# First loads split and reordered, x turned tile by tile into eight banks, second bias summed in four row groups, ple inputs turned in the routing stage

## Chip, cores, metric

One core of a Trainium2 chip. The metric is the device time of one execution in microseconds. TensorE is called PE, VectorE DVE, ScalarE ACT, GpSimd POOL and SyncE SP.

## What is computed

One hybrid layer on 256 prompt tokens and 8 samples of 8 tokens (320 tokens, model width 1024, all float32), with a final norm. Cut to what matters:

```
h = rmsnorm(x, norm1_g);  z = h @ w_in              # 8208 columns, cut into the inputs of the branches
qkv, new_buf = short_conv(qkv_pre, conv_buf, conv_w)  # conv_buf: the last 3 rows of every sample
y_a = gated delta rule branch;  y_b = chunk MLP branch
x = x + (sigmoid(m_a) * y_a + sigmoid(m_b) * y_b) @ w_out
h2 = rmsnorm(x, norm2_g)
x = x + moe_ffn(h2)      # 32 experts, top 4, blocks of 64 rows; each block: act(xe @ w1[e] + b1[e]) @ w2[e] + b2[e], times its gate
h3 = rmsnorm(x, norm3_g)
x = x + sigmoid(h3 @ ple_gate_w) * (p @ ple_w)
y = rmsnorm(x, final_norm_g)
```

Because the gates multiply b2[e] too, the kernel adds it once for all tokens: gates (tokens x 32) times b2 (32 x 1024).

## The kernel before

The program is written engine by engine, with semaphores set by hand. All of SBUF is one array ("arena") in which regions are used again in later stages; PSUM is one array ps of 8 banks of 512 words, and pj[0], pj[1] are its banks 0 and 1. Tokens form three tiles: two of 128 (prompt) and one of 64 (samples).

**Start.** SP issues its loads in one queue (L407 to L421): x (prompt, samples), all constants (725 KB, the identity matrix in their first 128 columns), the small rows that are transposed into per-partition columns (conv_w, three norm gains, dn_norm_g), the convolution state (288 KB), then the first 2 MB chunk of w_in, the small gate weights with two broadcasts, and the second chunk. Every later chunk waits until the chunk two before it has been used (L423 to L426). ACT takes the sum of squares of each tile (rms), DVE normalises it (L1441 to L1450) and copies the turned rows out of PSUM (L1451). PE waits for constants and rows (L645, L646), turns the rows (L647), then the convolution state in 24 transposes of 24 rows (L648 to L652), then x: for each of 8 blocks of 128 columns three transposes, one per tile, into bank k % 2, and ACT or DVE copies each bank out, scaled by norm1_g, into hT (L1204, L1456). So block k waits until block k - 2 has been copied:

```
            for k in range(KD):
                ...
                elif k >= 2:
                    pe.wait_ge(sem(("hT_ready", "hT_odd_ready")[k % 2]), k // 2)
                for tt, (t0, tn) in enumerate(TILES):
                    m = pe.transpose(pj[k % 2][:, t0:t0 + tn], x[0:tn, tt, k * P:(k + 1) * P], ident[0:tn, 0:tn])
```

When hT is complete (L690, L691), 24 feature products follow (L692), each of 8 matmuls of 320 columns; a float32 matmul is two passes in the trace. POOL, ACT and DVE do the short convolution behind them. All products go through the helper at L642.

**Middle.** The rest of the projections runs between the steps of the delta rule. SP reloads x for the residual (L459, L460) just before the chunks of w_proj_b (L461). In the routing stage (L938 to L988) h2 is transposed, the router logits are computed (bank 7) and transposed, x is put into banks 0 to 4 by identity products (L961, L1089) as the start of the output sum, and DVE works out ranks, block tables and gates. gmT (L1817) holds the gates with experts on 32 partitions. SP then waits for the tables (L486) and issues the loads of the experts' weights, each waiting for the slot to be used (L489 to L495).

**Expert blocks.** For each block of 64 rows PE does the select, hidden, second product and combine; combine (L995) adds a block's rows to banks 0 to 4 as 18 bfloat16 matmuls.

**End.** After the last block SP loads ple_gate_w and ple_w (L499 to L504), then b2, the ple inputs and the final norm gain (L506 to L509), which share one semaphore. PE waits for them (L1107), does the products of gates and b2 (L1108 to L1112, K = 32 rows), the last combine (L1113), and turns the ple inputs (L1115 to L1118). DVE copies the sum out of PSUM (L1865 to L1868), the norm of each tile follows (samples first), PE turns it (turn_h3, L1143), and the ple products (L1135) and gate logits (L1138) are done in the order of L1153 to L1179. ACT and DVE close with sigmoid, product, norm and store.

## Time and profile before

| what | value |
|---|---|
| median of 3 runs | 1649.81 us (1649.1 to 1650.41) |
| the profiled execution | 1651.6 us, span 1649.8 us |
| PE busy | 1595.5 us (97%) |
| DVE, ACT, POOL busy | 518.9, 327.0, 105.1 us |
| DMA | 477.23 MB, mean 289 GB/s |
| mean granted PE clock | 0.987 |

The profile gives times from the span's start. A busy PE is not PE at its peak, so the rows further on give counts of passes with their time, and the chain of waits tells what each stretch ended on. Matmuls and weight loads (PEld) overlap.

### The profile page before, as it was taken

The page shows a single profiled execution, that of the slowest core. Times are in us where ns is not written, and L with a number is a line of the kernel's source. Part 1 is how long each engine was busy: PE and PEld are TensorE (multiplying, and loading weights), DVE is VectorE, ACT ScalarE, POOL GpSimd, SP SyncE. Part 2 cuts the span into 40 slices and gives each one's busy share as a digit, 9 for nine tenths or more (in the row PEclk, how much of TensorE's full clock was granted, in tenths as well). Part 3 has the DMA queues.
Part 4 walks back from the last instruction along what each step waited for, and adds up shares of the span by engine and source line. Part 5 has one row for each costly group of instructions (what it writes and reads, how often), then busy time and mean ns, then how long its engine had stood idle before and what let it go on. Part 6 is the DMA issues. An engine that isn't in the chain of part 4 may idle for free.

```text
span 1649.8 us, 21617 instructions
## 1 busy us (share of the span) xinstructions
PE 1595.5 (97%) x8645; PEld 750.2 (45%) x8646; DVE 518.9 (31%) x1110; ACT 327.0 (20%) x529; POOL 105.1 (6%) x150
## 2 busy tenths in 40 slices
PE   7999999999999999999999999999999999999998
PEld 4667776676575433333333333333333333333333
DVE  3665322134561422222222222222122222222223
ACT  2224222122410131111111111111111111111123
POOL 1321202011103030000000000000000000000000
PEclk9999999999899999999999999999999999999989
DMA  5234321216574659996999999999999969949930
GB/s 162 103 111 135 97 77 56 99 62 207 168 231 148 273 229 427 429 428 262 424 430 427 430 427 429 429 427 430 427 429 428 427 288 407 430 198 419 422 106 32
DMA packets 71936, 477.23 MB, mean 289 GB/s; under 512 B 7914, under 2 KB 18595, under 8 KB 47235
## 3 DMA queue, kind: packets, MB, share of 16 engines
q1 hardware_dynamic: 69414, 467.65, 69.6%
q0 software_dynamic: 2480, 8.98, 1.9%
q8 instruction: 31, 0.51, 0.1%
q14 instruction: 11, 0.09, 0.0%
HBM read 469.73 MB, written 6.62 MB: 289 GB/s over the span
## 4 chain that ended last, share of the span: by engine, by line
PE 73%; DMA 21%; DVE 3%; issue 1%; SPq 1%; ACT 0%; DVEq 0%
PE ps L642 69%; DMA arena<-in_moe_w 20%; PE ps L992 1%; PE ps L1067 1%; PE ps L1012 1%; DMA arena<-in_final_norm_g 1%; DVE arena L1597 1%; PE ps L660 0%; DMA arena<-in_state_conv 0%; DVE arena L1631 0%; DVE arena L1594 0%; PE ps L714 0%; DVE arena L1635 0%; SPq L503 0%; DVE arena L1661 0%
## 5 line engine op out<-in xcount | busy, mean ns | idle before, releaser
L642 PE MATMUL ps<-arena 128*64 128x512 f32 (+9 forms) x8056 | 1499.3, 463 | 31.5 <-DMA arena<-in_moe_w 15.6
L642 PEld LDWEIGHTS ps<-arena 128*64 128x64 f32 (+7 forms) x8056 | 675.8, 143 | 815.9 <-issue 599.8
L1848 DVE TENSOR_SCALAR arena<-ps 128x512 f32<-128x512 f32 x35 | 24.2, 692 | 354.8 <-PE ps L642 354.8
L1395 ACT ACTIVATE arena<-arena 128x512 f32<-128x512 f32 x35 | 22.0, 630 | 413.9 <-DVE arena L1848 413.9
L1401 ACT ACTIVATE arena<-ps,arena 128x512 bf16<-128x512 f32 x35 | 24.1, 688 | 283.2 <-PE ps L642 283.2
L1861 DVE SCALAR_TENSOR_TENSOR arena<-ps,arena 128x512 f32<-128x512 f32 x35 | 26.3, 751 | 126.8 <-ACT arena L1401 126.8
L1820 DVE TENSOR_TENSOR arena<-ps,arena 128x512 f32<-128x512 f32 x36 | 24.9, 692 | 128.7 <-PE ps L992 128.7
L1856 DVE TENSOR_REDUCE arena<-ps 128x1 f32<-128x320 f32 x35 | 17.2, 492 | 95.8 <-PE ps L1012 95.8
L1395 ACT ACT_TABLE_LOAD x35 | 44.9, 1283 | 0.6
L1380 ACT ACTIVATE arena<-ps 128x512 f32<-128x512 f32 x36 | 21.6, 599 | 109.0 <-PE ps L642 109.0
L1481 DVE SCALAR_TENSOR_TENSOR arena<-arena 128x344 f32<-128x344 f32 x48 | 35.6, 741 | 1.7
L1263 ACT ACTIVATE arena<-ps 128x320 f32<-128x320 f32 x32 | 14.0, 436 | 98.3 <-PE ps L642 98.1
L992 PEld LDWEIGHTS ps<-arena 128*128 128x128 f32 x144 | 19.9, 207 | 28.5 <-issue 28.4
L1193 ACT ACTIVATE arena<-arena 128x1024 f32<-128x1024 f32 (+1 forms) x12 | 12.6, 1051 | 97.5 <-DVE arena L1716 91.1
L1863 DVE TENSOR_TENSOR arena<-arena 128x512 bf16<-128x512 f32 x35 | 24.2, 693 | 24.4 <-ACT arena L1403 24.4
L1843 DVE TENSOR_SCALAR arena<-arena 128x128 f32<-128x128 f32 (+1 forms) x105 | 29.6, 337 | 0.0
L1403 ACT ACTIVATE arena<-arena 128x512 bf16<-128x512 f32 x35 | 22.0, 630 | 28.6 <-DVE arena L1861 28.6
L992 PE MATMUL ps<-arena 128*128 128x128 f32 x144 | 26.9, 309 | 0.0
L1575 DVE TENSOR_TENSOR arena<-arena,ps 128x512 f32<-128x512 f32 (+1 forms) x11 | 7.6, 688 | 59.8 <-PE ps L642 59.8
L1067 PE MATMUL ps<-arena 128*128 128x128 f32 x140 | 26.2, 310 | 0.0
L1851 DVE SCALAR_TENSOR_TENSOR arena<-arena 128x512 f32<-128x512 f32 x35 | 24.3, 694 | 1.2
L1854 DVE TENSOR_TENSOR arena<-arena 128x512 f32<-128x512 f32 x35 | 24.3, 693 | 1.2
(256 smaller groups left out, 699.8 us busy)
## 6 DMA issues: line engine op xcount, KB each, us to landing
arena<-in_moe_w SPq DMA_DIRECT2D x192, 2048.0 KB, 19.5
arena<-in_w_in SPq DMA_DIRECT2D x16, 2048.0 KB, 11.0
arena<-in_state_delta POOLq DMA_DIRECT2D x16, 512.0 KB, 6.4
arena<-in_w_proj_a SPq DMA_DIRECT2D x2, 2048.0 KB, 11.1
out_sd_s<-arena SPq DMA_DIRECT2D x8, 512.0 KB, 5.7
arena<-in_w_proj_b SPq DMA_DIRECT2D x2, 2048.0 KB, 11.3
arena<-in_w_out SPq DMA_DIRECT2D x2, 2048.0 KB, 8.0
arena<-in_ple_gate_w SPq DMA_DIRECT2D x2, 2048.0 KB, 15.1
```

Source lines behind the costliest of these rows:

```text
L642: return pe.matmul(out, lhsT, rhs, start=first, stop=last, skip_group_check=True)
L992: m = pe.transpose(ps[:, TURN_B, P * j:P * j + P], xsel_by_k[:, j // 2, j % 2, :], ident)
L1067: m = pe.transpose(ps[:, GATE_B, P * j:P * j + P], a_by_k[:, j, :], ident)
L1395: ACTF(s_sb, g_sb, ACT.Sigmoid, scale=ALPHA).then_inc(sem("glu_sig_ready"), 1)
L1481: ch.link(STT(a, z[:, i:i + CW], g_conv[:, i, n:n + 1], a, ALU.mult, ALU.add))
L1820: TT(xselT.rearrange("p (g j) s -> p g j s", g=2), ps[:, TURN_B, :].rearrange("p (j g s) -> p g j s", j=4, g=2), g2_by_k.rearrange("p (g j ...
L1843: m = TS(Pg[0:tn, tt, :], cst("slot", tn), posb[0:tn, tt, bass.ds(b, 1)], gateb[0:tn, tt, bass.ds(b, 1)], ALU.is_equal, ALU.mult)
L1848: TS(g_sb, ps[:, GATE_B, :], LIMIT, None, ALU.min).then_inc(sem("glu_gate_ready"), 1)
L1851: STT(u_sb, u_sb, 1.0, g_sb, ALU.add, ALU.mult).then_inc(sem("glu_up_ready"), 1)
L1854: TT(a_sb, u_sb, s_sb, ALU.mult).then_inc(sem("act_ready"), 1)
L1861: STT(y_rest, ps[:, UP_B, :], gate_col, y_parts[0], ALU.mult, ALU.subtract).then_inc(sem("ysb_ready"), 1)
L1863: TT(y_parts[2], y_rest, y_parts[1], ALU.subtract).then_inc(sem("ysb_ready"), 1)
```

## The change

At the start x is loaded in three loads with a semaphore each, and only the identity's 128 columns of the constants go ahead; the convolution state and the rest of the constants go behind the first weight chunk, the small gate weights behind the second. PE turns x tile by tile, each block k into bank k, behind the turned rows; the convolution state is turned in groups of four transposes behind products 0 to 5. The first product waits block by block for hT.

The ple inputs and the final norm gain are loaded before x is loaded again, and turned in the routing stage into banks 0 and 1; the identity products take tile 1 first. b2 is loaded four times, to partitions 0, 32, 64 and 96, after the tables are ready, and gmT is copied to the same groups. At the end the b2 products of the two prompt tiles use a row group each; ple products 0, 4 and 1 go around the last combine, and 2 and 3 later.

```diff
-            sp.dma_start(x[:, 0:2, :], t["x_prompt"][0].rearrange("(a p) d -> p a d", p=P)).then_inc(sem("x_in"), 16)
-            sp.dma_start(x[0:64, 2, :], t["x_sample"].rearrange("b s d -> (b s) d")).then_inc(sem("x_in"), 16)
-            sp.dma_start(arena[:, cst_at:cst_at + NCONST], t["consts"]).then_inc(sem("consts_in"), 16)
+            for tt in range(2):
+                sp.dma_start(x[:, tt, :], t["x_prompt"][0, P * tt:P * tt + P, :]).then_inc(sem(f"x_tile{tt}_in"), 16)
+            sp.dma_start(x[0:64, 2, :], t["x_sample"].rearrange("b s d -> (b s) d")).then_inc(sem("x_tile2_in"), 16)
+            sp.dma_start(arena[:, cst_at:cst_at + P], t["consts"][:, 0:P]).then_inc(sem("ident_in"), 16)
...
-            sp.dma_start(sc_rows[0:24, :], t["state_conv"][0].rearrange("b r n -> (b r) n")).then_inc(sem("rows_loaded"), 16)
             for c in range(FRONT_SLOTS):
                 sp.dma_start(slots[c], chunk_src[c]).then_inc(landed[c], 16)
                 if c == 0:
-                    sp.dma_start(wab, w_in[:, :, COL_AB:COL_AB + 16]).then_inc(sem("ab_in"), 16)
-                    sp.dma_start(alog, t["a_log"].broadcast_to([P, H])).then_inc(sem("ab_in"), 16)
-                    sp.dma_start(dtb, t["dt_bias"].broadcast_to([P, H])).then_inc(sem("ab_in"), 16)
+                    sp.dma_start(sc_rows[0:24, :], t["state_conv"][0].rearrange("b r n -> (b r) n")).then_inc(sem("consts_in"), 16)
+                    sp.dma_start(arena[:, cst_at + P:cst_at + NCONST], t["consts"][:, P:NCONST]).then_inc(sem("consts_in"), 16)
+            sp.dma_start(wab, w_in[:, :, COL_AB:COL_AB + 16]).then_inc(sem("ab_in"), 16)
+            sp.dma_start(alog, t["a_log"].broadcast_to([P, H])).then_inc(sem("ab_in"), 16)
+            sp.dma_start(dtb, t["dt_bias"].broadcast_to([P, H])).then_inc(sem("ab_in"), 16)
...
+            sp.wait_ge(sem("S0_stored2"), 32)
+            sp.dma_start(ptok[:, 0:2, :], t["p_prompt"][0, 0].rearrange("(a p) d -> p a d", p=P)).then_inc(sem("ple_in"), 16)
+            sp.dma_start(ptok[0:64, 2, :], t["p_sample"][0].rearrange("b s d -> (b s) d")).then_inc(sem("ple_in"), 16)
+            sp.dma_start(fng, t["final_norm_g"].rearrange("(a d) -> a d", a=1).broadcast_to([P, D])).then_inc(sem("ple_in"), 16)
+            sp.dma_start(x[:, 0:2, :], t["x_prompt"][0].rearrange("(a p) d -> p a d", p=P)).then_inc(sem("x_tile0_in"), 16)
+            sp.dma_start(x[0:64, 2, :], t["x_sample"].rearrange("b s d -> (b s) d")).then_inc(sem("x_tile2_in"), 16)
...
             sp.wait_ge(sem("tables_ready"), 1)
+            for i in range(4):
+                sp.dma_start(b2[32 * i:32 * i + 32, :], t["moe_b2"][0]).then_inc(sem("router_in"), 16)
...
-            sp.wait_ge(used[uslot[3]], nb)
-            sp.dma_start(b2[0:NE, :], t["moe_b2"][0]).then_inc(sem("ple_in"), 16)
-            sp.dma_start(ptok[:, 0:2, :], t["p_prompt"][0, 0].rearrange("(a p) d -> p a d", p=P)).then_inc(sem("ple_in"), 16)
-            sp.dma_start(ptok[0:64, 2, :], t["p_sample"][0].rearrange("b s d -> (b s) d")).then_inc(sem("ple_in"), 16)
-            sp.dma_start(fng, t["final_norm_g"].rearrange("(a d) -> a d", a=1).broadcast_to([P, D])).then_inc(sem("ple_in"), 16)
...
-            pe.wait_ge(sem("consts_in"), 16)
-            pe.wait_ge(sem("rows_loaded"), 16 * 6)
-            pe.transpose(pj[1][:, 0:121], rows_in[0:121, :], ident[0:121, 0:121]).then_inc(sem("rows_turned"), 1)
-            for g in range(6):
+            pe.wait_ge(sem("ident_in"), 16)
+            pe.wait_ge(sem("rows_loaded"), 16 * 5)
+            pe.transpose(ps[:, 7, 384:505], rows_in[0:121, :], ident[0:121, 0:121]).then_inc(sem("rows_turned"), 1)
+            for tt, (t0, tn) in enumerate(TILES):
+                pe.wait_ge(sem("xn_ready"), tt + 1)
+                for k in range(KD):
+                    if tt == 0 and k == 7:
+                        pe.wait_ge(sem("cols_ready"), 1)
+                    m = pe.transpose(ps[:, k, t0:t0 + tn], x[0:tn, tt, k * P:(k + 1) * P], ident[0:tn, 0:tn])
+                    if tt == 2:
+                        m.then_inc(sem("hT_done"), 1)
+
+            def turn_old(g):
+
+                if g == 0:
+                    pe.wait_ge(sem("consts_in"), 32)
                 for i in range(4):
                     f = 4 * g + i
                     m = pe.transpose(ps[:, 2 + g, 24 * i:24 * i + 24], sc_rows[0:24, f * P:(f + 1) * P], ident[0:24, 0:24])
-                m.then_inc(sem("old_done"), 1)
-            pe.wait_ge(sem("xn_ready"), 3)
-            for k in range(KD):
-                if k == 1:
-                    pe.wait_ge(sem("cols_ready"), 1)
-                elif k >= 2:
-                    pe.wait_ge(sem(("hT_ready", "hT_odd_ready")[k % 2]), k // 2)
-                for tt, (t0, tn) in enumerate(TILES):
-                    m = pe.transpose(pj[k % 2][:, t0:t0 + tn], x[0:tn, tt, k * P:(k + 1) * P], ident[0:tn, 0:tn])
-                m.then_inc(sem("hT_done"), 1)
+                m.then_inc(sem("rows_turned"), 1)
...
                 for k in ks:
+                    if n == 0:
+                        pe.wait_ge(sem(("hT_ready", "hT_odd_ready")[k % 2]), k // 2 + 1)
                     last = mm(pj[n % 2][:, 0:TOK], slots[c % FRONT_SLOTS][:, k, m * P:(m + 1) * P], rhs[:, k, :], k == 0, k == KD - 1)
...
-            pe.wait_ge(sem("hT_ready"), KD // 2)
-            pe.wait_ge(sem("hT_odd_ready"), KD // 2)
             for n in range(FT):
                 features(n, n // 4, n % 4, hT)
+                if n < 6:
+                    turn_old(n)
...
+            def turn_p(k):
+
+                for tt, (t0, tn) in enumerate(TILES):
+                    m = pe.transpose(ps[:, P_BANKS[k], t0:t0 + tn], ptok[0:tn, tt, k * P:(k + 1) * P], ident[0:tn, 0:tn])
+                m.then_inc(sem("pT_done"), 1)
+
+            pe.wait_ge(sem("ple_in"), 48)
+            turn_p(0)
             pe.wait_ge(sem("hT_odd_ready"), KD + 1)
             for k in range(KD):
                 m = mm(ps[0:NE, 7, SEQ:TOK], rw[:, k, :], h2T[:, k, SEQ:TOK], k == 0, k == KD - 1)
             m.then_inc(sem("logits_done"), 1)
+            turn_p(1)
             pe.wait_ge(sem("logitT_ready"), 1)
             for tt, (t0, tn) in enumerate(TILES):
                 m = pe.transpose(ps[0:tn, 6, NE * tt:NE * tt + NE], logitT[0:NE, t0:t0 + tn], ident[0:NE, 0:NE])
             m.then_inc(sem("logits_done"), 1)
 
-            for tt in range(2):
+            for tt in (1, 0):
+                if tt == 0:
+                    pe.wait_ge(sem("pT_ready"), 2)
                 for g in range(2):
                     mm(ps[:, 2 * tt + g, :], ident, x[:, tt, 512 * g:512 * g + 512], True, True)
...
-            pe.wait_ge(sem("ple_in"), 64)
-            for tt in range(2):
-                for g in range(2):
-                    mm(ps[:, 2 * tt + g, :], gmT[0:NE, P * tt:P * tt + P], b2[0:NE, 512 * g:512 * g + 512], False, True)
-            for g in range(2):
-                mm(ps[64 * g:64 * g + 64, 4, :], gmT[0:NE, 2 * P:TOK], b2[0:NE, 512 * g:512 * g + 512], False, True)
-            combine(nb + 1)
-            pe.wait_ge(sem("xselT_ready"), nb + 1)
-            for k in range(2):
-                for tt, (t0, tn) in enumerate(TILES):
-                    m = pe.transpose(ps[:, P_BANKS[k], t0:t0 + tn], ptok[0:tn, tt, k * P:(k + 1) * P], ident[0:tn, 0:tn])
-            m.then_inc(sem("pT_done"), 1)
...
-            pe.wait_ge(sem("pT_ready"), 2)
+            pe.wait_ge(sem("router_in"), 16 * 8)
+            pe.wait_ge(sem("rankT_ready"), 3)
+            for tt in range(2):
+                for g in range(2):
+                    q = 32 * (2 * tt + g)
+                    mm(ps[:, 2 * tt + g, :], gmT[q:q + NE, P * tt:P * tt + P], b2[q:q + NE, 512 * g:512 * g + 512], False, True)
+            for g in range(2):
+                mm(ps[64 * g:64 * g + 64, 4, :], gmT[0:NE, 2 * P:TOK], b2[0:NE, 512 * g:512 * g + 512], False, True)
+            ple_product(0)
+            combine(nb + 1)
             ple_product(4)
+            ple_product(1)
             pe.wait_ge(sem("xn_ready"), 7)
             turn_h3(2)
-            ple_product(0)
             for half in range(2):
                 pe.wait_ge(landed[uslot[half]], 16 * (before[uslot[half]] + NE + 1))
             pe.wait_ge(sem("hT_odd_ready"), KD + 2)
             pe.wait_ge(sem("xn_ready"), 8)
             turn_h3(0)
             gate_logits(4, range(KD // 2, KD))
-            ple_product(1)
+            ple_product(2)
             pe.wait_ge(sem("hT_odd_ready"), KD + 4)
             gate_logits(0)
             pe.wait_ge(sem("ple_added"), 1)
             pe.wait_ge(sem("xn_ready"), 9)
             turn_h3(1)
-            ple_product(2)
             ple_product(3)
```

DVE copies the turned rows before tile 1's norm, copies a group of the convolution state before its convolution of product n < 6 (keep_old), and copies gmT to partitions 32, 64 and 96 after the tables. ACT copies the turned ple inputs before the exponential of the gates (L1375).

## Rows read from the trace of the kernel before

**Rows 1.** The page: the chain that ended last, shares of the span.

```profile
PE 73%; DMA 21%; DVE 3%; issue 1%; SPq 1%; ACT 0%; DVEq 0%
```

**Rows 2.** Chain of the first 60 us: start, duration (us), what.

```profile
4.49 7.03 DMA arena<-in_state_conv
...
12.09 2.68 PE ps L651 x24
14.77 7.31 PE ps L660 x24
...
22.77 37.44 PE ps L642 x127
```

**Rows 3.** Timeline of the first 45 us: start, duration, what, idle before.

```profile
1.84 0.57 SPq L409 DMA_DIRECT2D arena<-in_consts  x1
...
4.83 0.40 SPq L417 DMA_DIRECT2D arena<-in_w_in  x1
...
23.43 0.34 PEld L642 LDWEIGHTS ps<-arena 128*128 128x128 f32 x1 [0.20 <-issue]
...
28.74 16.39 PEld L642 LDWEIGHTS ps<-arena 128*128 128x128 f32 x61 [0.17 <-issue]
```

**Rows 4.** Timeline of the last 110 us: start, duration, what, idle before.

```profile
1543.34 3.65 PE L642 MATMUL ps<-arena 128*64 128x512 f32 x16
...
1565.42 0.98 PEld L642 LDWEIGHTS ps<-arena 64*128 64x128 bf16 x12 [0.41 <-issue]
...
1567.60 1.22 PEld L642 LDWEIGHTS ps<-arena 128*64 128x64 bf16 x14 [0.41 <-issue]
...
1580.36 11.80 PE L642 MATMUL ps<-arena 32*128 32x512 f32 x30 [1.44 <-DMA arena<-in_final_norm_g]
...
1581.13 0.69 DVE L1863 TENSOR_TENSOR arena<-arena 128x512 bf16<-128x512 f32 x1 [0.69 <-ACT arena L1403]
...
1592.10 1.21 PE L1117 MATMUL ps<-arena 128*128 128x128 f32 x6
...
1597.09 0.71 PE L1149 MATMUL ps<-arena 64*128 64x64 f32 x8 [0.90 <-DVE arena L1446]
...
1603.23 1.09 PE L1149 MATMUL ps<-arena 128*128 128x128 f32 x8
...
1617.40 24.20 PE L642 MATMUL ps<-arena 128*128 128x512 f32 x56
```

**Rows 5.** Stretches: length, busy (count) of PE, PEld, DVE, ACT, POOL; clock, DMA, GB/s.

```profile
1581.60:1583.00 1.40, 1.40 (x3) 0.65 (x2) 0.23 (x1) 1.01 (x2) 0.00 (x0) 0.56 0.00 0
...
1590.00:1592.00 2.00, 2.00 (x10) 0.36 (x6) 0.00 (x0) 0.00 (x0) 0.00 (x0) 0.50 0.00 0
```

**Rows 6.** DMA issues of the first 60 us: KB each, us to landing.

```profile
arena<-in_w_in SPq DMA_DIRECT2D x3, 2048.0 KB, 11.8
...
arena<-in_consts SPq DMA_DIRECT2D x1, 725.5 KB, 7.5
```

**Rows 7.** Stretches at the start, columns as in rows 5.

```profile
12.00:13.00 1.00, 1.00 (x11) 0.98 (x10) 0.84 (x3) 0.00 (x0) 0.00 (x0) 1.00 1.04 383
```

**Rows 8.** Chain of the expert loop.

```profile
962.12 24.80 DMA arena<-in_moe_w
986.97 3.68 PE ps L642 x16
```

**Rows 9.** Timeline of SP's queue in the middle.

```profile
466.11 0.67 SPq L426 DMA_DIRECT2D arena<-in_w_proj_b  x1
...
487.32 0.37 SPq L426 DMA_DIRECT2D arena<-in_w_proj_b  x1
```

**Rows 10.** Timeline of the routing stage and the first block.

```profile
564.98 1.09 PE L642 MATMUL ps<-arena 128*32 128x64 f32 x16 [0.78 <-DVE arena L1737]
...
583.61 0.17 DVE L1830 CAST arena<-ps 1x32 int32<-1x32 f32 x1
...
595.19 15.92 SPq L495 DMA_DIRECT2D arena<-in_moe_w  x5
```

More of the change, by code:

```diff
@@ L310, in hybrid_layer @@
         ple_moved = y_rest[0:64]
-        assert mo[0] <= small_at, (mo[0], small_at)
+        print("margin", small_at-mo[0], "small", small_at+1100-sm[0]); assert mo[0] <= small_at, (mo[0], small_at)
         def part_of(tt, i):
@@ L1203, in _ @@
                 act.wait_ge(sem("hT_done"), k + 1)
-                ACTF(hT[:, k, :], pj[k % 2][:, 0:TOK], ACT.Copy, scale=g1[:, k:k + 1]).then_inc(sem("hT_ready"), 1)
+                ACTF(hT[:, k, :], ps[:, k, 0:TOK], ACT.Copy, scale=g1[:, k:k + 1]).then_inc(sem("hT_ready"), 1)
             def silu_part(n):
@@ L1373, in _ @@
             turned((4, 5))
+            for k in range(2):
+                act.wait_ge(sem("pT_done"), k + 1)
+                ACTF(pT[:, k, :], ps[:, P_BANKS[k], 0:TOK], ACT.Copy).then_inc(sem("pT_ready"), 1)
             act.wait_ge(sem("top_ready"), 1)
@@ L1406, in _ @@
             ACTF(warm, eps_col, ACT.Sqrt)
-            act.wait_ge(sem("pT_done"), 1)
-            for k in range(2):
-                ACTF(pT[:, k, :], ps[:, P_BANKS[k], 0:TOK], ACT.Copy).then_inc(sem("pT_ready"), 1)
             for i, tt in enumerate(TAIL_TILES):
@@ L1455, in _, with keep_old @@
                 dve.wait_ge(sem("hT_done"), k + 1)
-                TS(hT[:, k, :], pj[k % 2][:, 0:TOK], g1[:, k:k + 1], None, ALU.mult).then_inc(sem("hT_odd_ready"), 1)
-            for g in range(6):
-                dve.wait_ge(sem("old_done"), g + 1)
-                dve.tensor_copy(oldT[:, 4 * g:4 * g + 4, :], ps[:, 2 + g, 0:96].rearrange("p (f j) -> p f j", f=4)).then_inc(sem("old_turned"), 1)
+                TS(hT[:, k, :], ps[:, k, 0:TOK], g1[:, k:k + 1], None, ALU.mult).then_inc(sem("hT_odd_ready"), 1)
+            def keep_old(g):
+                dve.wait_ge(sem("rows_turned"), g + 2)
+                dve.tensor_copy(oldT[:, 4 * g:4 * g + 4, :], ps[:, 2 + g, 0:96].rearrange("p (f j) -> p f j", f=4)).then_inc(sem("cols_ready"), 1)
             def samples(w):
@@ L1473, in _ @@
             for n in range(FT):
+                if n < 6:
+                    keep_old(n)
                 evacuated(dve, n)
@@ L1834, in _ @@
             nb = dve.value_load(tab[0:1, 96 + NE - 1:96 + NE], min_val=1, max_val=MAXB)
+            for i in range(1, 4):
+                m = dve.tensor_copy(gmT[32 * i:32 * i + 32], gmT[0:32])
+            m.then_inc(sem("rankT_ready"), 1)
             dve.wait_ge(sem("part_ready"), 6)
```

30 lines of the change are left out of this document (14 added, 16 removed).

## The prediction

> **What bounds the kernel now.** I read the chain of waits first. Over the whole span it is TensorE for 73% and DMA for 21% [rows 1]. The edit sits at the two ends and in the routing stage, so the question for each part is what holds those stretches, and whether a shift of the start reaches the end.
>
> At the start PE does nothing until the last row load, the one of the convolution state, has landed; then come 24 small transposes (2.68 us), 24 transposes of x held back by two PSUM banks (7.31 us), and at 22.77 the first product. After that the chain is PE without a break past 60 us [rows 2]. The first products run slowly: a weight load of one pass takes 0.34 us after 0.20 idle, so one starts every 0.53, and from 28.74 on 61 of them take 16.39 us, 0.27 each [rows 3]. So the array is at 1.2 GHz until 28.7 and at 2.4 after it.
>
> At the end PE stands idle 1.44 us for the final norm gain's load, issued behind the bias and the ple inputs; the second bias and the last combine then run until 1592.1 [rows 4]. From 1581.8 on, the granted clock is 0.50, the lower level [rows 5]. After the combine comes a norm of the last tile that PE waits out, then a solid block of products, from 1617.40 for 24.2 us [rows 4].
>
> **The start, part by part.** (1) *Loads.* PE now waits for x, 64 KB of identity and the small rows instead of all constants and the convolution state. Constants landed 7.5 us after their issue at 1.84, so at 9.34 [rows 3, 6]; of their 725 KB 661 move away, 1.8 us at the 383 GB/s of a full stretch [rows 7]. I take the rows at 7.9 us: 9.34 less 1.8, plus a little for the split loads (7.5 to 9.4, the full saving or none). Their transpose ends near 8.35. The first weight chunk, 11.8 us after its issue at 4.83, landed at 16.6; 949 KB (constants' rest and convolution state) no longer precede it, 2.5 us, so it lands at 14.1, or up to 0.7 earlier.
>
> (2) *Turning x tile by tile into eight banks.* No transpose waits for a bank now. At 2.4 GHz eight full transposes took 1.09 us and eight 64-row ones 0.71 [rows 4]; at 1.2 GHz I double that: 2.2 + 2.2 + 1.4 = 5.8 us, so PE is through at 14.2. The gains' copy on DVE now stands ahead of tile 1's norm, which still has the 2.2 us of tile 0's transposes to hide in. The first product needs only bank 0's copy, which runs beside the other transposes. First product at 14.3 against 22.77: **8.5 us**.
>
> (3) *Clock.* Before, 5.9 us of products ran at half speed, a loss of 3.0. PE no longer pauses between transposes and products (7.31 after 14.77 is 22.08, then nothing until 22.77 [rows 2]), so I take 0.8 of it back, between -0.8 and 1.3.
>
> (4) *The old rows' transposes* move behind products 0 to 5, four each. At 1.2 GHz they took 2.68 us together. At 2.4 four cost 4 x 0.089 (0.71/8) = 0.36. To this comes the change of row shape: the six ple transposes took 1.21 us [rows 4] where four full and two short ones at the rates above are 4 x 0.136 + 2 x 0.089 = 0.72, so 0.49 for three changes, 0.16 each. Two changes per group, part of it already in the 0.71: 0.55 a group, **3.3 us back** (2.1 to 5). The Trainium skill, page "TensorEngine Tiling (Array Packing)", Tiling Modes, speaks against this part: changing the tiling mode drains the array. The trace agrees, with 0.16 us a change. What these groups wait for (constants' rest, convolution state, near 17) is there before product 0 ends, near 21. The second chunk, now issued right behind the first, is needed at product 4, near 35. The small gate weights behind it are needed at product 24.
>
> Start in sum: 8.5 + 0.8 - 3.3 = **6.0 us**. It carries to the end if the rest moves with it. The one long DMA-bound stretch (from 962, twelve or thirteen experts of 25.5 us DMA and 3.7 PE each [rows 8]) is paced by slots that PE frees; I expect it to shift whole.
>
> **The middle.** On SP the ple inputs and the norm gain (832 KB, three issues) now go ahead of the reload of x and of w_proj_b. That is 2.2 us at 383 GB/s, with the issues 3 to 4 us, for a chunk issued at 466.11; PE needs it when its neighbour is issued, at 487.3 [rows 9]. With 11.8 us for landing it comes at 482: hidden, 5 us over. What queues behind the new wait for a stored state is this same chunk. Turning p (six transposes, 1.21 us) goes into PE's idle time: 0.78 us before 564.98 [rows 10], and a gap while the logits are copied. ACT copies it before an exponential that waits for DVE. I count 0.1 us lost (0 to 0.8). Three copies of gmT run on DVE while it waits for parts. The four loads of b2 follow the tables at 583.8, when SP has nothing until 595.19 [rows 10]: 512 KB, 1.4 us, over before the first expert load. If they did collide, one stall of 1.4 us would appear in the expert loop.
>
> **The end.** PE's last expert product lets the next begin at 1578.85.
> - b2: four full products in a row are 4 x 2 x 0.43 = 3.4 us at 2.4 GHz (56 passes in 24.20). On four row groups I let them run together, as two column halves do: 16 passes in 3.65, 0.23 each [rows 4]. So 0.9 for the four, 0.9 for the sample pair, 0.1 of change. The Trainium skill, "TensorE: Matmul & The Clock Gate", Part 3, gives 3.07 times for four row tiles, not four: the sum would be 0.2 less.
> - ple product 0: 4 x 0.43 = 1.7. Combine may start at 1582.5; its last part is ready at 1581.8 (1581.13 + 0.69), so no idle time.
> - combine at 2.4 GHz: 1565.42 to 1567.60 [rows 4], 2.2 us, and 0.2 of drain. It ends at 1584.9 instead of 1592.1: 7.2 us (wait 1.5, clock 5.0, packing 2.4, less 1.7 put in).
> - The last tile's norm takes 5.0 us as before (1592.1 to 1597.09). PE fills 3.5 of it with ple products 4 and 1; h3's transposes start at 1589.9.
> - Before, ple product 0 (1.7 us) stood behind them; now the logits wait only for DVE's copy, 0.8 us. Together 8.1.
> - One product fewer stands in the rest: 1.7. Together **9.8 us**. ACT's and DVE's closing 8 us stay.
>
> **Sum.** 6.0 - 0.1 + 9.8 = 15.7. The profiled execution took 1651.6, 1.8 outside its span, and would take 1635.9. It stands 1.8 above the median of 1649.8; less 15.7 that gives 1634.1, so **1634.0**.
>
> **Rivals.**
> - *The clock falls in the new gap at the end.* PE now stands idle 1.3 us before the h3 transposes and 0.8 after them. Before, an idle 1.44 us followed by 32-row products preceded the fall [rows 4, 5]. Against: gaps around the same transposes did not lower it before (0.90 ahead of them), and the packed products fill more of the array. A third of the 10.2 us seen costs 1.7, the whole 5.1: 1635.7 to 1639. Chance 0.30.
> - *One end pays less.* Row groups serial (2.5), old-row transposes at their upper bound (1.7), rows landing at 9.4 (1.5): 1639.7 together; or the start's gain is lost whole because DMA paces the experts [rows 8]: 1640. Against: those loads wait for PE. 0.15.
> - *Slower.* The small transposes behind each of the first six products could keep the array at 1.2 GHz, as it was through all transposes before 22 [rows 2, 3]. Six products are 6 x 16 passes of 0.27, 26 us; at half speed 26 more, 2.2 of them counted: 1634 + 23.8 = 1658. It decides if the low clock lasts beyond some 35 us after the first product. Against: each product is 4.3 us without a gap. 0.02.
> - *The edit does nothing there*, since something else held PE: 0.02; the chain names both loads.
>
> **Chances.** Forecast 0.51, clock at the end 0.30, a gain missed 0.15, same 0.02, slower 0.02. 0.2% is 3.3 us, about what runs of this kernel tell from no change; all cases but the last two are faster by more. The range runs from 1629.5 (rows and chunk early 1.0, clock 0.5, old rows at 2.1 another 1.2, and half-speed stretches elsewhere that may shorten as work shifts, 1.8) to 1640.0 (the clock falls, or a gain missed).
>
> **What would show it.** First product near 14.3, with nothing waiting for the convolution state; its pace 0.27 by 20; groups of four small transposes of 0.5 us; no wait of PE for the norm gain; clock 1.00 from 1560 to the last logits; four b2 products together; expert loads where they were against the tables. Wrong if PE waits for the weight chunk at the start, if a DMA wait is new in the expert loop, or if the combine still runs at 0.50.

## The result, and the profile after

The changed kernel took 1640.53 us (median of four runs, 1638.59 to 1642.08), the kernel before 1650.11 beside it (1649.1 to 1650.53): ratio 0.9953, interval 0.9936 to 0.9971. Forecast were 1634.0 and a range from 1629.5 to 1640.0. The direction is right; of 15.7 us forecast 9.6 came. Later, on another chip, the same two gave 1637.57 and 1646.73, ratio 0.9938 (0.9925 to 0.9952).

The profiled execution took 1640.53 (span 1638.7; before 1651.6 and 1649.8). From here on A is the kernel before and B the changed one. The timeline of B's start, columns as in [rows 3]:

```profile
4.71 0.42 SPq L416 DMA_DIRECT2D arena<-in_w_in  x1
5.17 0.53 SPq L418 DMA_DIRECT2D arena<-in_state_conv  x1
5.74 0.53 SPq L419 DMA_DIRECT2D arena<-in_consts  x1
6.32 1.35 SPq L416 DMA_DIRECT2D arena<-in_w_in  x1
7.71 8.78 SPq L420 DMA_DIRECT2D arena<-in_w_in  x1
8.05 0.43 PE L649 MATMUL ps<-arena 121*128 121x121 f32 x1 [8.05 <-DMA arena<-in_dn_norm_g]
8.29 4.53 PE L655 MATMUL ps<-arena 128*128 128x128 f32 x24
12.42 1.93 DVE L1469 TENSOR_SCALAR arena<-ps,arena 128x320 f32<-128x320 f32 x4 [1.91 <-PE ps L655]
18.00 6.92 PE L644 MATMUL ps<-arena 128*128 128x320 f32 x16 [5.19 <-DMA arena<-in_w_in]
24.85 0.42 PE L665 MATMUL ps<-arena 24*128 24x24 f32 x4
...
29.72 0.43 PE L665 MATMUL ps<-arena 24*128 24x24 f32 x4
```

The small rows came at 8.05, close to the forecast 7.9, and x was turned by 12.8, earlier than the forecast 14.2. Then PE stands idle for 5.19 us, for the first weight chunk. The chain of the start says the same:

```profile
4.71 13.25 DMA arena<-in_w_in
...
18.00 6.92 PE ps L644 x16
```

The chunk landed 13.25 us after its issue, at 17.96: later than before (16.6, [rows 3, 6]), though 949 KB that went ahead of it now stand behind it. DMA traffic in two stretches of before and then of after (columns as in [rows 5]; the last two are the busy share of the DMA engines and GB/s; the clock column reads 1.00 up to the first recorded change, in B at 12.5, so ahead of that the clock's level is read from the pace of the passes):

```profile
7.00:11.00 4.00, 0.00 (x0) 0.00 (x0) 1.52 (x4) 3.45 (x7) 0.00 (x0) 1.00 1.02 287
...
14.00:18.00 4.00, 4.00 (x19) 2.34 (x18) 0.55 (x1) 0.98 (x2) 0.00 (x0) 1.00 0.53 173
```

```profile
7.00:11.00 4.00, 2.94 (x14) 2.98 (x15) 1.92 (x5) 1.38 (x3) 0.00 (x0) 1.00 0.61 211
...
14.00:18.00 4.00, 0.00 (x0) 0.00 (x1) 0.35 (x1) 0.09 (x1) 0.00 (x0) 0.74 0.92 237
```

After the change the engines are only 0.61 busy just when the chunk should stream, and busy with it and its followers when PE waits.

The end, PE's timeline:

```profile
1572.24 13.61 PE L644 MATMUL ps<-arena 128*64 128x512 f32 x62
1586.99 0.71 PE L1154 MATMUL ps<-arena 64*128 64x64 f32 x8 [1.14 <-DVE arena L1459]
1588.57 5.35 PE L644 MATMUL ps<-arena 128*64 128x512 f32 x16 [0.88 <-DVE arena L1898]
...
1608.02 22.48 PE L644 MATMUL ps<-arena 128*128 128x512 f32 x52
```

Its weight loads show the second bias and the combine:

```profile
1575.83 0.31 PEld L644 LDWEIGHTS ps<-arena 32*128 32x128 f32 x8 [0.81 <-issue]
1576.90 0.19 PEld L644 LDWEIGHTS ps<-arena 32*64 32x64 f32 x4 [0.76 <-issue]
1577.90 0.30 PEld L644 LDWEIGHTS ps<-arena 128*128 128x128 f32 x2 [0.81 <-issue]
...
1579.82 0.98 PEld L644 LDWEIGHTS ps<-arena 64*128 64x128 bf16 x12 [0.76 <-issue]
```

And the clock ahead of h3's transposes and behind them:

```profile
1582.00:1588.00 6.00, 4.56 (x22) 1.73 (x20) 4.90 (x7) 4.33 (x10) 0.00 (x0) 1.00 0.00 0
1589.50:1592.80 3.30, 3.30 (x10) 1.14 (x8) 0.00 (x0) 0.00 (x0) 0.00 (x0) 0.50 0.00 0
```

The wait for the norm gain is gone (PE has no idle time ahead of the products at 1575.83); the four bias products take 1.07 us together; the combine runs at full clock from 1579.82. But behind the two idle spells (1.14 and 0.88 us) the clock falls for 3.4 us: sixteen logit passes take 5.35 us instead of the 3.65 of [rows 4].

**Splitting the difference.** The expert stage makes a good mark: the second expert whose weights PE waits for. In before and after:

```profile
1016.34 3.87 PE L642 MATMUL ps<-arena 128*64 128x512 f32 x18 [1.24 <-DMA arena<-in_moe_w]
```

```profile
1013.18 8.23 PE L644 MATMUL ps<-arena 128*64 128x512 f32 x54 [1.24 <-DMA arena<-in_moe_w]
```

Ahead of it the change brought 3.2 us, behind it (633.5 against 625.5 us to the end of the span) 8.0. The same marks of every profile taken (times in us; the mark is the same expert in all):

| profile | first product | second expert wait | from there to end | span |
|---|---|---|---|---|
| A | 22.77 | 1016.34 | 633.5 | 1649.8 |
| A again (e12) | 22.34 | 1014.31 | 633.8 | 1648.1 |
| A third (e13) | 22.12 | 1014.62 | 632.7 | 1647.3 |
| B | 18.00 | 1013.18 | 625.5 | 1638.7 |
| B again (e11) | 17.93 | 1013.18 | 623.6 | 1636.8 |
| B, chunk held alone (e1) | 15.61 | 1013.22 | 625.2 | 1638.4 |
| B, second chunk held (e2) | 17.83 | 1011.50 | 623.7 | 1635.2 |
| B, old rows together (e3) | 18.27 | 1011.59 | 625.3 | 1636.9 |
| B, spells filled (e4) | 19.52 | 1016.77 | 623.7 | 1640.5 |
| the same again (e14) | 18.01 | 1010.84 | 623.8 | 1634.6 |
| B, chunk on ACT's queue (e5) | 19.10 | 1013.06 | 625.3 | 1638.4 |
| three edits (e6) | 18.95 | 1009.27 | 622.9 | 1632.2 |
| B, bias in one row group (e7) | 17.98 | 1010.70 | 627.9 | 1638.6 |
| B's end, A's start (e8) | 22.81 | 1015.45 | 625.5 | 1641.0 |
| held, together, split (e9) | 15.52 | 1008.61 | 622.9 | 1631.5 |
| e9 with halves (e10) | 13.02 | 1008.16 | 622.9 | 1631.1 |

Two things stand in it. In B and its variants the part behind the mark repeats to 0.3 us once it is known whether the clock fell (623.6 to 623.8 without, 625.2 to 625.5 with). The part ahead of it does not: five profiles of B's start (B, B again, e4, e7, e14) lie between 1010.7 and 1016.8. In them the low-clock stretches between 100 and 700 us add up to 24 to 31 us, near the same places but of 3.4, 6.8 or 10.2 us each; with the chunk's landing (18.0 to 19.5) that is part of the spread, not all of it.

### The profile page after: what moved, and what is told of

It is laid out like the page before. It is cut to its first block, busy times and chain, and to the rows that moved or that the text cites. A ratio compares the mean times of both kernels' runs of the same rounds, so it can differ in the third digit from the quotient of the medians.

```text
span 1638.7 us, 21626 instructions
## 1 busy us (share of the span) xinstructions
PE 1586.7 (97%) x8645; PEld 747.7 (46%) x8646; DVE 521.3 (32%) x1113; ACT 327.5 (20%) x529; POOL 105.1 (6%) x150
## 4 chain that ended last, share of the span: by engine, by line
PE 74%; DMA 21%; DVE 3%; issue 1%; ACT 0%; SPq 0%; DVEq 0%
PE ps L644 70%; DMA arena<-in_moe_w 20%; PE ps L1010 1%; PE ps L1085 1%; PE ps L1030 1%; DMA arena<-in_w_in 1%; DVE arena L1612 1%; DVE arena L1646 0%; DVE arena L1609 0%; PE ps L721 0%; DVE arena L1650 0%; DVE arena L1676 0%; DVE arena L1658 0%; DVE arena L1656 0%; PE ps L835 0%
## 5 line engine op out<-in xcount | busy, mean ns | idle before, releaser
L644 PE MATMUL ps<-arena 128*64 128x512 f32 (+9 forms) x8056 | 1494.9, 463 | 33.1 <-DMA arena<-in_moe_w 15.1
L1233 ACT ACTIVATE arena<-ps 128x64 f32<-128x64 f32 x24 | 5.5, 230 | 95.7 <-PE ps L644 95.7
## 6 DMA issues: line engine op xcount, KB each, us to landing
arena<-in_ple_gate_w SPq DMA_DIRECT2D x2, 2048.0 KB, 15.1
```

The source lines that it names most:

```text
L644: return pe.matmul(out, lhsT, rhs, start=first, stop=last, skip_group_check=True)
```

## The experiments

Theory: (1) the chunk came late since what is issued behind it takes from it; rival: a chunk is slow by itself, whatever stands behind it; (2) the clock fell because of the two idle spells.

**e1: everything behind the first chunk waits for it.**

```diff
                 sp.dma_start(slots[c], chunk_src[c]).then_inc(landed[c], 16)
                 if c == 0:
+                    sp.wait_ge(landed[0], 16)
```

> The queue now waits for the first weight chunk before it issues the convolution state, the rest of the constants, the second chunk and all that follows. Theory A (what is issued behind the chunk takes part of the DMA engines while it loads): the chunk lands near 14.2, which is its issue at 4.71 and some 9.5 us, the first product starts near 14.3 and not at 18.00, 3.7 us earlier; the old rows' transposes then wait for the late state and constants (949 KB, issued at 14.3, there near 19), 1 to 2 us given back. Total 1638 to 1640 against 1640.5 of the changed kernel. Theory B (the pace at which one chunk's own 1024 packets of 2 KB go out is what sets its landing, about 11 us as for other weight chunks of this kernel): lands at 15.7 to 16, first product near 16, and after the wait for the old rows no gain in the total. Theory C (nothing behind it matters): 18.0 as now, total longer by 2 us or more.

**e2: only the second chunk and the gate weights wait** (the same line behind the constants' load).

> Only the second weight chunk and the small loads behind it wait for the first chunk; the convolution state and the rest of the constants (949 KB) are issued right behind the first chunk as in the changed kernel. If it was the state and the constants that delayed the first chunk: lands near 17.9 as now. If it was the second chunk and the gate weights: near 14.2 to 15, first product 3 us earlier, old rows there in time, total near 1637.5. If both share: between, near 16.5, total near 1639.

Measured: e1 1638.48 us (0.9927, 0.9902 to 0.9952), e2 1636.86 (0.9929, 0.9908 to 0.9949). PE's timeline in e1 and a stretch of it:

```profile
15.61 7.45 PE L645 MATMUL ps<-arena 128*128 128x320 f32 x16 [3.16 <-DMA arena<-in_w_in]
...
7.00:11.00 4.00, 2.59 (x13) 2.62 (x14) 1.92 (x5) 1.90 (x6) 0.00 (x0) 1.00 0.64 236
```

and in e2:

```profile
17.83 6.72 PE L645 MATMUL ps<-arena 128*128 128x320 f32 x16 [5.20 <-DMA arena<-in_w_in]
```

With nothing behind it the chunk landed 10.9 us after its issue, at 15.6 (15.5 in e9); with state and constants behind it, at 17.8; with the second chunk too, at 17.9 to 18.2 in five profiles and 19.5 in e4's. So both are true: state and constants behind it cost it 2.2 us, the second chunk mostly little (0.1 to 0.4, once 1.7), and alone it is still 1.5 us later than I had forecast. Against the kernel before, whose chunk landed 11.8 us after its issue with the 949 KB in front, taking them away brought 1.0 us and not 2.5. The record of the kernel before could have told this. From its page:

```profile
arena<-in_w_in SPq DMA_DIRECT2D x16, 2048.0 KB, 11.0
```

Fourteen of these sixteen chunks are issued one by one from 43 us on, and none of them landed in less than 9.7 us. What sets this pace is open. In e1 the last small rows landed at 8.4; from then to 11 the chunk is alone and the DMA engines are 0.61 busy at 229 GB/s, and from 11 to 14, still alone, they are 0.90 busy:

```profile
11.00:14.00 3.00, 1.45 (x14) 1.14 (x13) 1.82 (x4) 1.78 (x4) 0.00 (x0) 1.00 0.90 322
```

So the chunk does not go out at one pace, and no run here says why it starts slowly. The Trainium skill, page "DMA: Bandwidth & Descriptors", section "Anatomy of one DMA — SWDGE (gpsimd) path", has a fit of 2.0 us plus bytes over 436 GB/s for loads issued by GpSimd; for 2 MB that is an estimate of 6.8 us, and this load, issued by SP, took 10.9.

In e1 the lead of 2.4 us over B is gone at the second expert wait. Product 0 gives back 0.5 (7.45 us, 5.8 of it at the low clock). The conv rows' transposes take 5.00 against 4.49, which undoes 0.35 gained just before them. At 208 us PE stands idle 0.4 us, as it does not in B, and 1.3 of the lead is left. Some 1.0 reaches the first expert for whose weights PE waits:

```profile
983.80 8.23 PE L644 MATMUL ps<-arena 128*64 128x512 f32 x54 [0.23 <-DMA arena<-in_moe_w]
```

```profile
983.85 8.24 PE L645 MATMUL ps<-arena 128*64 128x512 f32 x54 [1.24 <-DMA arena<-in_moe_w]
```

The first line is B's, the second e1's: PE comes earlier and waits 1.0 us longer. It would be easy to say that the experts' loads take up to a microsecond of a shift, but that is not shown: over all profiles the wait there lies between 0 and 1.24 us, and e4, whose PE comes latest of the variants of B, waits 1.24 as well.

**e3: the old rows turned together, behind product 0.**

```diff
-                if n < 6:
-                    turn_old(n)
+                if n == 0:
+                    for g in range(6):
+                        turn_old(g)
```

> All 24 transposes of the old rows stand behind product 0 in one group, in place of four behind each of the products 0 to 5. If the 0.6 us of a group is mostly the change between full tiles and 24-row tiles (four transposes alone 0.36, so 0.25 a group), five changes go: 1.2 us shorter, 1639.3. If it is the transposes and their weight loads themselves, no difference: 1640.5. If DVE, which has to copy all six groups one by one, or the low clock (products 0 runs at 1.2 GHz until 22.8, the transposes after it too) makes them dearer, longer by up to 2 us.

Measured: 1635.74 us (0.992, 0.9903 to 0.9938). PE's timeline:

```profile
25.31 1.70 PE L665 MATMUL ps<-arena 24*128 24x24 f32 x24
26.93 9.44 PE L644 MATMUL ps<-arena 128*128 128x320 f32 x34
```

All 24 take 1.62 us to the next product. One by one, the groups start 4.87 us apart (24.85, 29.72), against 4.27 for the 16 passes of a product at 0.267 each (61 in 16.39 in [rows 3], the last one's end counted in), so 0.60 each, 3.6 for six. Together they save 2.0 us, more than the 1.2 expected: of a group of four, 0.4 is the two changes of shape and only 0.2 the transposes. At the mark e3 is 1.6 us ahead of B, which is within the spread.

**e5: the first chunk issued on ACT's queue at 0.72**, state and constants behind the rows, the second chunk held.

```diff
+            act.dma_start(slots[0], chunk_src[0]).then_inc(landed[0], 16)
             act.wait_ge(sem("zeroed"), 4)
```

> The first weight chunk is issued on ACT's queue as that engine's first instruction (near 0.7 us in place of 4.71 on SP's), beside the loads of x; the state and the rest of the constants follow the rows on SP, the second chunk and the gate weights wait for the first. Theory B (a chunk needs about 11 us for its own packets: 10.9 with nothing behind it, where 16.6 of before is 11.8 behind its issue): it lands 11 to 13 us after its issue, so at 12 to 14, though it shares the engines with x, which comes perhaps 2 us later; the first product starts at 13.5 to 15, bound by the turning of x, in place of 18.0 to 19.5. Total 3 to 4 us below the changed kernel, 1636.5 to 1637.5. Rival (bytes: x, chunk, state and constants are 4.4 MB, at 383 GB/s all there at some 13.5 however ordered, but x comes later with the chunk beside it): x's turning ends 3 us later, near 16, and the first product starts near 16; total 1638.5.

Measured: 1637.22 us (0.9947, 0.9927 to 0.9966), no better than B. ACT's queue, the DMA issues of the first 16 us (KB, us to landing), and PE:

```profile
0.72 0.48 ACTq L1208 DMA_DIRECT2D arena<-in_w_in  x1
...
arena<-in_w_in ACTq DMA_DIRECT2D x1, 2048.0 KB, 17.3
...
14.19 0.43 PE L648 MATMUL ps<-arena 121*128 121x121 f32 x1 [14.19 <-DMA arena<-in_dn_norm_g]
...
19.10 4.56 PE L643 MATMUL ps<-arena 128*128 128x320 f32 x16 [0.34 <-ACT arena L1217]
```

Issued four microseconds earlier, the chunk landed at 18.0 as ever, and the small rows came at 14.19 instead of 8.05. This is worse than my rival had it: the chunk took 17.3 us beside the other loads, and delayed them. The Trainium skill, "DMA: Bandwidth & Descriptors", "Issuing engines are not separate DMA queues", says that DMAs of different issuing engines run on the same 16 DMA engines and interleave; the trace agrees. Product 0 does run at full clock here (4.56 us): the first recorded rise is at 18.2, ahead of it, and PE stands idle only 0.34 us between. It is no rule that a product right behind the transposes does so: in e10 further on the rise comes at 17.1, and product 0, from 13.02, takes 6.59 us.

**e4, e14: both idle spells filled**: four products of 256 columns, overwritten afterwards, ahead of ple product 1, whose second half moves behind the last tile's transposes.

```diff
+            for i in range(4):
+                mm(ps[:, PLE_BANKS[1], 0:256], pT[:, 0, 0:P], wp[:, 0, 0:256], True, True)
-            ple_product(1)
+            ple_product(1, (0,))
             pe.wait_ge(sem("xn_ready"), 7)
             turn_h3(2)
+            ple_product(1, (1,))
```

> PE's two idle spells around the last tile's transposes (1.14 us before them, 0.88 after) are filled: four products of 256 columns that are overwritten afterwards stand before ple product 1, and its second half stands behind the transposes. The work added is 1.7 us, all of it in idle time. If the fall of the clock at 1589.5 in the changed kernel follows from these idle spells: the granted clock stays at 1.00 until the last logits, the first 16 logit products take 3.65 us and not 5.35, and the total is 1.7 less up to 0.3 for the filler, 1638.8 to 1639.1. Rival: the fall comes from elsewhere (the 32-row products of the second bias, some 10 us before it): the clock falls as now, total 1640.5 to 1641.

> The kernel with both idle spells around the last tile's transposes filled, again. Of nine profiles whose end keeps both spells (1.14 and 0.88 us of PE idle), the clock fell behind them in five (changed kernel, and the runs with the loads held back, the old rows together, the chunk on ACT's queue, and the end alone), and not in three more, in one of which it fell earlier. In the four with the spells filled, or one of them filled and the other 0.94, it fell in none. If the spells are the cause: none here, 1.00 from 590 to the end, and from the second expert wait to the end of the span 623.7 us as in the first run of this kernel. If it was chance: a fall between 1585 and 1595 can be here as well, and 625.4.

Measured: 1639.93 us (0.9944, 0.9926 to 0.9962) and 1637.75 (0.9953, 0.9931 to 0.9975). Timeline of e4, and its clock over this place:

```profile
1590.42 0.71 PE L1157 MATMUL ps<-arena 64*128 64x64 f32 x8 [0.27 <-DVE arena L1465]
1591.07 4.71 PE L644 MATMUL ps<-arena 128*128 128x512 f32 x18
...
1588.00:1596.00 8.00, 7.73 (x38) 3.40 (x37) 3.76 (x7) 4.38 (x10) 0.00 (x0) 1.00 0.00 0
```

The clock stays at 1.00 in both, and from the mark to the end they take 623.7 and 623.8 us. With the spells left in, the eight profiles with B's order divide: the fall came in B, e1, e3, e5 and e8, not in B again and e2 (623.6 and 623.7) nor in e7, where the clock fell earlier. With the spells filled or one of them taken out (e4, e14, e6, e9, e10) none fell. Five of eight against none of five would come by chance once in 23 times. So it is likely, and not proven, that the spells allow the fall; they do not force it. It costs 1.8 us. The total does not show it: the part ahead of the mark varies by more (1016.77 and 1010.84 in these two).

**e7: all four bias products in row group 0** (`q = 0`).

> The four full products of the second bias all take their 32 rows from row group 0, in place of one row group each; the sample pair as before. The same instructions and bytes. If the four in different row groups run together: here they run one after the other, 4 x 2 x 0.43 = 3.4 us in place of 0.9 to 1.1, so the combine starts 2.4 us later (near 1582.2 against 1579.8 in the trace), and so does everything behind it: 1643 against 1640.5. Rival: the four did not overlap in time and the gain at this place came from the bias being there early: no difference, 1640.5.

Measured: 1641.99 us (0.9969, 0.9956 to 0.9981). PE's weight loads, first and last of the four and the sample pair, and a stretch right behind them:

```profile
1573.20 0.29 PEld L644 LDWEIGHTS ps<-arena 32*128 32x128 f32 x2 [0.81 <-issue]
...
1576.84 0.19 PEld L644 LDWEIGHTS ps<-arena 32*64 32x64 f32 x4 [0.76 <-issue]
...
1577.90:1581.00 3.10, 3.10 (x6) 1.12 (x4) 0.00 (x0) 0.00 (x0) 0.00 (x0) 0.50 0.00 0
```

The four take 3.64 us instead of 1.07: 2.6 us, as reckoned. That is 3.4 times, where my sum had four products run fully together. The Trainium skill, "TensorE: Matmul & The Clock Gate", Part 3, gives 3.07 for four row tiles; the measured ratio is above it. And the clock falls at 1577.8, with no idle spell in front, in this one profile; in the kernel before the same products stood behind an idle 1.44 us. From the mark to the end it is 627.9, 4.3 us over B again: 2.6 for the products and 1.7 for the clock. So row groups may have brought more than the prediction booked to them.

**e8: A's start, B's routing stage and end.**

> The start is that of the kernel before (loads in its order, x turned by two banks, old rows ahead of all), the routing stage and the end are those of the changed kernel. By the two traces the start brought 2.6 us and the end 8.1 (9.8 where the clock does not fall in its gap): 1649.8 less 8.1 to 9.8, 1640 to 1641.7. Rival: part of what I read as the end's gain is a shift that the experts' stage passes on from the start (3.0 before it, 2.6 at the start): then the end alone brings 7.7. A first product at 22.8 and the first expert's first wait near 987 are to be seen in both.

Measured: 1639.42 us (0.995, 0.9936 to 0.9964). The mark at 1015.45 and 625.5 us behind it: what comes behind the mark belongs to the end and owes nothing to the start. By the total the start's part can't be told from nothing: the end alone has the ratio 0.9950, the whole change 0.9953 and 0.9938.

**e6, e9, e10: three edits together.** At the end ple product 0 goes half ahead of the combine, half behind it:

```diff
-            ple_product(0)
+            ple_product(0, (0,))
             combine(nb + 1)
+            ple_product(0, (1,))
             ple_product(4)
-            ple_product(1)
+            ple_product(1, (0,))
             pe.wait_ge(sem("xn_ready"), 7)
             turn_h3(2)
+            ple_product(1, (1,))
```

e6 adds e3's and e5's edits to this, e9 e3's and e1's; e10 is e9 with the first chunk in two loads of four k each, and product 0 waits for the second half at k = 4.

> Three edits together: the first chunk on ACT's queue with the second held back; the old rows turned in one group behind product 0 (alone: the stretch from the first product to the first transposes of the conv rows shortened from 124.1 to 121.4 us); at the end, ple product 0 in two halves, one ahead of the combine and one behind it, and the second half of product 1 behind the last tile's transposes. The combine starts 0.86 us earlier, unless its last part is late; the norm and the transposes of h3 with it; the second idle spell of PE (0.88 us) is filled. If the parts add: 3.5 + 2.7 + 0.9 us below the changed kernel, and the clock stays up more often at the end (1.7 us where it does): 1633 to 1634, ratio to before 0.990. If the start is paced by x instead: 1635 to 1636. If the shift is swallowed by the experts' loads (429 GB/s without a gap): no better than 1637.

> Three edits that each did what it should alone: state, constants, second chunk and gate weights behind the first chunk's landing (it landed at 15.6 in place of 18.0); the old rows turned in one group (2.7 us less up to the conv rows' transposes); ple product 0 in two halves around the combine, the second half of product 1 behind the last tile's transposes (from the second expert wait to the end 622.9 us in place of 625.5, 1.7 of it the clock). If the parts add: first product at 15.6, the second expert that waits for its weights at 1013.2 less 2.4 and 2.7, near 1008, less or more up to 3 by the low-clock stretches of the middle, and 623 from there: span 1631, time 1633, 7 us below the changed kernel run beside it, ratio to before 0.989 to 0.991. If the late state and constants hold the old rows' group: PE waits up to 1 us for them behind product 0, and the gain is 6. If the chunk's landing is not worth what it brings, since the low clock then falls on more of product 0: 5.

> As the run before, with the first weight chunk in two loads, rows k 0 to 3 and 4 to 7; product 0 starts with the first half and waits again before its fifth pass. If a chunk goes out at its own pace from the moment x has gone (6.1 to 15.6, 9.5 us for 1024 packets), half of it is there near 11 to 11.5, and what then sets product 0's start is the turning of x and its first copy, 12.8 to 14.3; its second half starts at 15.6. So product 0 begins near 14 and ends 1.5 to 2.3 us earlier than with one load. If packets of both loads go side by side: the first half lands near 15 too, no difference.

Measured: e6 1635.16 us (0.9933, 0.9914 to 0.9951); beside B, e9 1633.11 (0.9911, 0.9896 to 0.9926) and e10 1633.34 (0.9916, 0.9902 to 0.9929). Timeline of e10:

```profile
8.33 4.67 PE L659 MATMUL ps<-arena 128*128 128x128 f32 x24
13.02 6.59 PE L648 MATMUL ps<-arena 128*128 128x320 f32 x16
20.84 1.69 PE L669 MATMUL ps<-arena 24*128 24x24 f32 x24 [1.23 <-DMA arena<-in_consts]
```

e6 was to come near a ratio of 0.990 and did not; its start is e5's, which had brought nothing. The tail gives 622.9 us from the mark in all three, 0.7 under B again. e10's product 0 starts at 13.02, right behind the transposes, and PE then waits 1.23 us for the constants, which were held back: 2.5 us earlier than e9 at the first product, 2.0 behind the old rows, 0.45 at the mark, nothing in the total. Most of the lead goes between 133 and 140 us, where the clock is low for 6.8 us in e10 and for 3.4 in e9. e9 is the best kernel here with e10: 4.5 us under B on the same chip.

**e11, e12, e13: B and A unaltered.**

> The changed kernel again, unaltered, beside the two others on the same chip. It measures how far executions of the same code lie apart: in the runs so far its own start code gave a first product at 18.0, 18.0 and 19.5 and the second expert wait at 1010.7 to 1016.8. If that spread comes from the low-clock stretches (each 3.4 or 6.8 us long, at the same few places of the middle) and from the chunk's landing, this run's marks lie within it, 1010 to 1017, and the median within 1636 to 1642.

> The kernel before, unaltered. Its executions on other chips lie in two groups, near 1645.5 and near 1650, and the profiled one (1651.6) is of the upper. If the low clock at its end (0.50 from 1581.76 to 1592.00, 5 us of products lost) comes in every execution, it is to be seen here too, and the groups have another cause. If it is a matter of the execution: it is absent or shorter in a profile whose span is near 1644 to 1645, and of the 5.0 us that the prediction gave to the clock a part was only this execution's.

> The kernel before once more, for the same question: two more profiles of the same code. A span near 1649.8 with the low clock at the combine, or one near 1645 without it; if spans differ by over 2 us and the low clock at the end does not, the middle's low-clock stretches (3.4 or 6.8 us at four places) make the difference.

Measured: B 1637.57 us; A 1647.88 and 1649.22 (ratios 1.0004 and 1.001 to A's other runs). All three profiles of A show the low clock ahead of the combine and through it, 10.2 us long; here the second:

```profile
1580.00:1592.00 12.00, 11.83 (x35) 3.41 (x33) 1.38 (x2) 0.74 (x3) 0.00 (x0) 0.57 0.00 0
```

The two groups of A's times stay (1644.8 to 1645.6 and 1647.8 to 1650.7 in these two runs), and their mean granted clocks differ: 0.990 in all five executions of the lower group, 0.986 to 0.989 in those of the upper. 0.004 of 1648 us is 6.6 us of full clock, so the lower group had up to 13 us less of the low one (an estimate from these figures). Which stretches those are, the 10.2 at the combine among them or not, is open, since no profile fell in the lower group.

## Why the prediction was right or wrong

**Loads.** Rows at 7.9, transpose to 8.35, x turned by 14.2: measured 8.05, 8.48 and 12.8. The rows are right. x came earlier because I had doubled the transposes' time for the low clock, to 5.8 us; B again, whose first recorded rise of the clock is at 23.8, turned x in 4.67, and B, with a rise at 12.5, in 4.53.

**First weight chunk: the step that failed.** That 949 KB "no longer precede it, 2.5 us, so it lands at 14.1" took the landing for a sum of bytes in front. It landed at 17.96. With nothing behind it, it takes 10.9 us from its issue (e1), and the bytes gone from in front brought 1.0 us, not 2.5; state and constants behind it add 2.2 us (e2), the second chunk 0.1 and more. The change had moved state and constants behind the chunk and the second chunk up to them, and the sum had both at nothing there. First product at 18.00, 4.8 us gained of 8.5 forecast: 3.7 short. The prediction named this wait as what would make it wrong, but gave it no chance of its own.

**Clock at the start.** 0.8 taken back was forecast. Before, 5.9 us of products ran at half speed, now 4.8 (18.00 to 22.76): 0.6. Right in size, partly by luck: in B the clock rose during x's turning and fell again while PE waited for the chunk; in B again products ran 5.9 us at half speed, nothing taken back, and in e14 2.9.

**Old rows.** 0.55 a group forecast, 0.60 measured: 3.6 against 3.3. Two changes cost 0.4 and not 0.3 (e3). The rule of the Trainium skill, page "TensorEngine Tiling (Array Packing)", "Tiling Modes", that a change of tiling mode drains the array spoke against this part. The runs bear it out: one group of 24 in place of six of four is worth 2.0 us, more than half of what the part gives back.

**Start in sum.** 4.8 + 0.6 - 3.6 = 1.8 by these terms, against 6.0. The two profiles differ by 3.2 at the second expert wait; means over the five profiles of B's start and the four of A's there are 1012.9 and 1015.2, so 2.3, with executions of B up to 6 apart.

**Middle.** Nothing of the moved loads is to be seen: PE waits 15.1 us for experts' weights in 13 waits, 15.6 before. Right. Whether the start's gain carries through the experts whole is open: the wait at the first such expert varies by 1.24 us between executions. e9, with the best start but one, is 4.6 us ahead of B at the mark.

**End.** 9.8 us forecast; behind the mark 8.0 in the first pair of profiles, 9.9 (633.5 less 623.6) where the clock does not fall. Term by term: the bias products took 1.07 us, forecast 0.9 and 0.1 for the change; the combine was to start at 1582.5, and started at 1579.82, which is that less the 3.0 by which the last experts had moved, and 0.3 late; h3's transposes followed 7.2 us behind its start, forecast 7.4. Right.

**Rival 1 came true**, at 0.30: the clock fell behind the new idle spells, one third of the length before, for 1.8 us (1.7 forecast). It did so in B's first profile and not in its second. For the end's gain it matters too that A lost 5.1 us to its low clock there in all three profiles, but perhaps not in its faster executions, as said above.

**Sum.** 3.7 at the chunk, 0.2 at the start's clock, 0.3 at the old rows and 1.8 at the end's clock are 6.0 of the 15.7, which leaves 9.7. The medians differ by 9.6 and 9.2. The first pair of profiles differs by 11.1, and the 1.4 over lie ahead of the mark, where executions of one kernel differ by more; that the terms come so near the medians is partly luck. A's profiled execution was among its slowest (1651.6; the others lie from 1643.1 to 1652.5), and the median that I started from (1649.8, three runs) is above the 1646.6 to 1649.3 of A's later medians. The time lies 0.5 us above the range on the first chip and within it on the other (1637.57); in both the chunk's 3.7 are missing, and a case of its own for the chunk would have widened the range by about as much.

## What to carry to other kernels

A load's landing is not a sum of the bytes in front of it. It took 10.9 us by itself here, and what was issued behind it came on top: before moving loads, read in the trace how long one such load takes when it is alone, and ask whether what goes behind it can wait until it has landed. Small tiles of another shape strewn between large products cost more by their number of changes (0.4 us a group here) than by their work (0.2); put them together. Idle spells of a microsecond on PE may cost a second time by a fall of the clock behind them (1.8 us here, in five of eight profiles), and halves of independent products can fill them.

## What I had not expected of the hardware

- Four products of 32 rows in different row groups take 1.07 us, in one row group 3.64; and in one row group the clock fell behind them for 3.4 us though PE had not been idle (e7, from 1577.8, one profile). In every profile of the kernel before, where they stood behind an idle spell of 1.4 to 2.0 us, it fell for 10.2 us.
- The clock rose while x was being turned, ahead of any product (first recorded rise at 12.5 in B's profile, product 0 at 18.00), so transposes alone can raise it, and not in every execution: in B again the first rise is at 23.8.
- One 2 MB load of 2 KB rows, with nothing beside it, kept the DMA engines 0.61 busy at 229 GB/s from 8.5 to 11 us and 0.90 busy at 322 from 11 to 14 (e1), while the experts' loads run at 429 GB/s.
- The same kernel's marks before the experts lie up to 6 us apart from one execution to the next (1010.70 and 1016.77), more than most of the edits here are worth. Comparing sections of the profile between marks showed effects of 1 us that the totals hid.
